# Filling five layer norms of a two-block transformer with quarters of a projection or value product

## What is computed

```python
for i in range(DEPTH):                       # first block
    m = mla_mixer(x, ...) if i % 2 == 0 else gla_mixer(x, ...)
    x = layer_norm(DN_ALPHA * x + m, ln1_g[i], ln1_b[i])
    x = layer_norm(DN_ALPHA * x + conv_ffn(x, ...), ln2_g[i], ln2_b[i])
    gate = jax.nn.sigmoid(x @ ple_w_gate[i] + ple_b_gate[i])
    x = x + gate * (p[i] @ ple_w_proj[i])    # the projection: needs p alone
...
for l in range(DEPTH):                       # second block
    h = layer_norm_2(DEEPNORM_ALPHA * h + 0.5 * swiglu(h, ...), ...)
    mix = short_conv(h, ...) if l < N_A else forgetting_attention(h, w_q, w_o, k, v, c)
    h = layer_norm_2(DEEPNORM_ALPHA * h + mix, ...)
    h = layer_norm_2(DEEPNORM_ALPHA * h + 0.5 * swiglu(h, ...), ...)
    if l == N_A - 1:
        k, v, c = shared_kv(h, kv_w, f_bias) # used by the attention of layer 1
```

## Time and profile before

| | us |
|---|---|
| median of 3 runs | 1794.31 (1794.29 to 1795.25) |
| the profiled execution, its own time | 1793.77 |
| its span, first to last instruction | 1791.9 |
| mean granted clock of TensorE, share of full | 0.999 |

### The profile page before, as it was taken

The page is one execution under the profiler, slowest core; times in us unless marked ns, Lnnn a source line. Parts: engine busy times, 40 slices in busy tenths (PEclk is TensorE's granted clock), DMA queues, the critical chain, the costliest instruction groups (busy, mean ns, idle before and its releaser), DMA issues.

```text
span 1791.9 us, 32993 instructions
## 1 busy us (share of the span) xinstructions
PE 1770.7 (99%) x14168; PEld 1735.1 (97%) x14168; DVE 1134.4 (63%) x1835; ACT 969.8 (54%) x1531; POOL 117.9 (7%) x124
## 2 busy tenths in 40 slices
PE   8999999999999999999999999999999999999998
PEld 8999999997899999999999999999999999899998
DVE  6776888565479885755546665554655556765554
ACT  5665766466367664744435454443554444764443
POOL 1001000110020001100011020001100002020002
PEclk9999999999999999999999999999999999999999
DMA  6424455544345555455444445555444554245552
GB/s 213 144 95 153 170 182 185 187 166 158 125 142 193 186 186 186 155 185 176 177 176 153 173 143 182 176 176 177 153 170 165 188 184 158 95 162 182 186 188 95
DMA packets 85056, 297.74 MB, mean 166 GB/s; under 512 B 10512, under 2 KB 13456, under 8 KB 84912
## 3 DMA queue, kind: packets, MB, share of 16 engines
q1 hardware_dynamic: 84176, 294.85, 47.2%
q10 hardware_dynamic: 736, 0.80, 0.1%
HBM read 294.57 MB, written 1.05 MB: 165 GB/s over the span
## 4 chain that ended last, share of the span: by engine, by line
PE 92%; DVE 3%; ACT 2%; DMA 1%; issue 1%; SPq 0%; POOL 0%; ACTq 0%; DVEq 0%; POOLq 0%
PE ps L1433 27%; PE ps L1431 27%; PE ps L1432 27%; PE ps L1462 2%; PE ps L1467 2%; PE ps L1463 2%; PE ps L1484 1%; DVE w_lo L888 1%; PE ps L1442 1%; DMA par<-params 1%; PE ps L1699 1%; PE ps L1701 1%; ACT x L462 1%; ACT w_hi L424 0%; PE ps L1898 0%
## 5 line engine op out<-in xcount | busy, mean ns | idle before, releaser
L888 DVE TENSOR_TENSOR w_lo<-raw,w_hi 128x1024 fp32r<-128x1024 f32 x557 | 689.6, 1246 | 348.7 <-ACT w_hi L424 226.6
L424 ACT ACTIVATE w_hi<-raw 128x1024 fp32r<-128x1024 f32 x557 | 580.6, 1051 | 178.1 <-DMA raw<-stream 155.5
L1431 PE MATMUL ps<-a_hi,w_hi 128*128 128x256 f32 (+1 forms) x2088 | 595.5, 285 | 5.7 <-DVE w_lo L888 5.5
L1433 PE MATMUL ps<-a_hi,w_lo 128*128 128x256 f32 (+1 forms) x2088 | 592.9, 284 | 0.0
L1432 PE MATMUL ps<-a_lo,w_hi 128*128 128x256 f32 (+1 forms) x2088 | 592.4, 284 | 0.0
L1431 PEld LDWEIGHTS ps<-a_hi,w_hi 128*128 128x128 f32 x2088 | 394.9, 189 | 7.9 <-DVE w_lo L888 7.1
L1433 PEld LDWEIGHTS ps<-a_hi,w_lo 128*128 128x128 f32 x2088 | 395.3, 189 | 0.0
L1432 PEld LDWEIGHTS ps<-a_lo,w_hi 128*128 128x128 f32 x2088 | 393.3, 188 | 0.5
L1431 PE MATMUL ps<-h_hi,w_hi 128*128 128x256 f32 (+1 forms) x1336 | 379.4, 284 | 0.3 <-DVE w_lo L888 0.3
L1433 PE MATMUL ps<-h_hi,w_lo 128*128 128x256 f32 (+1 forms) x1336 | 378.0, 283 | 0.0
L1432 PE MATMUL ps<-h_lo,w_hi 128*128 128x256 f32 (+1 forms) x1336 | 377.4, 282 | 0.0
(11 more groups left out here) (266 smaller groups left out, 1855.8 us busy)
## 6 DMA issues: line engine op xcount, KB each, us to landing
raw<-stream SPq DMA_DIRECT2D x557, 512.0 KB, 3.3
x<-xT SPq DMA_DIRECT2D x2, 512.0 KB, 5.0
out<-x SPq DMA_DIRECT2D x8, 128.0 KB, 1.7
work<-pT ACTq DMA_DIRECT2D x2, 256.0 KB, 2.6
par<-params SPq DMA_DIRECT2D x1, 283.5 KB, 11.2
tmp<-causal ACTq DMA_DIRECT2D x1, 208.0 KB, 2.4
con<-consts SPq DMA_DIRECT2D x1, 194.5 KB, 9.5
tmp<-pos SPq DMA_DIRECT2D x1, 128.0 KB, 9.5
```

The lines of the kernel that those rows point to most:

```text
L424: nc.scalar.activation(w_hi[:, u % SLOTS, :], raw[:, u % SLOTS, :], ACT.Copy).then_inc(w_hi_ready, 1)
L888: nc.vector.tensor_tensor(w_lo[:, u % SLOTS, :], raw[:, u % SLOTS, :], w_hi[:, u % SLOTS, :].bitcast(F32), ALU.subtract).then_inc(w_lo_rea ...
L1431: nc.tensor.matmul(dst, wh, xh, start=first, stop=False, skip_group_check=True)
L1433: return nc.tensor.matmul(dst, wl, xh, start=False, stop=last, skip_group_check=True)
```

## The change

Five norms (mla, ffn0, gla, ffn1, ffn4) get one unit each in four quarters of six matmuls. The units `proj0` and `proj1` are parted: unit a goes from the end of the network into the norm mla or gla, unit b stays in ffn0 or ffn1. The eighth unit of `kv_v` goes into the norm ffn4 (`kv_w`); its values are turned and copied in the attention. In these norms keep_busy is gone, the order of the sums is another ("sums first"), and DVE takes the reciprocal ahead of the first subtraction (`covered`). p is loaded and split ahead of `mla_ob` and `gla_o`; the splits of the weights move one unit ahead there. POOL adds seven tiles in gla. Network 4 closes with two units like 0 and 1, and in all three the last residual stands ahead of the last `lo_next`.

```diff
-           ("kv_k", 8), ("kv_v", 8), ("kv_f", 1),
-           ("up4", 44), ("down4", 22), ("att_q", 8), ("att_o", 8), ("up5", 44), ("down5", 22)]
+           ("kv_k", 8), ("kv_v", 7), ("kv_f", 1),
+           ("up4", 44), ("down4", 22), ("kv_w", 1), ("att_q", 8), ("att_o", 8), ("up5", 44), ("down5", 22)]
...
+COVERED_FFNS = (0, 1, 4)
...
-        pooled_of = {name: 6 if name in ("gla", "att") else 7 for name in LN}
+        pooled_of = {name: 6 if name == "att" else 7 for name in LN}
...
@@ ACT, layer_norm @@
+                    if k == LN["ffn4"] and n in (0, 2, 4):
+                        act.wait_ge(late_read, n // 2 + 1)
...
@@ ACT, order of the stages @@
+            load_p(0)
             warm(ACT.Sqrt)
-            plain("mla_ob", LN["mla"], TOK)
+            plain("mla_ob", LN["mla"], TOK, 0)
             layer_norm(LN["mla"], TOK)
-
-            load_p(0)
+            projected(0, 0)
             ffn(0)
-            projected(0, 0)
-            layer_norm(LN["ffn0"], TOK, BASE["proj0"] + 1)
+            layer_norm(LN["ffn0"], TOK)
             projected(0, 1)
...
             layer_norm(LN["ffn4"], TOK)
+            nc.scalar.activation(vT[:, 1, :], ps[:, 4, 0:T], ACT.Copy).then_inc(vT_copied, 1)
             warm(ACT.Exp)
...
@@ DVE, layer_norm @@
-                dve.wait_ge(mean_spread, k + 1)
-                lessened = [less_mean(0)]
+                lessened = []
+                if not covered:
+                    dve.wait_ge(mean_spread, k + 1)
+                    lessened.append(less_mean(0))
                 dve.wait_ge(std_ready, k + 1)
                 nc.vector.reciprocal(spread, spread).then_inc(rstd_ready, 1)
-                lessened += [less_mean(1), less_mean(2)]
+                dve.wait_ge(mean_spread, k + 1)
+                for n in range(len(lessened), 2 if covered else 3):
+                    lessened.append(less_mean(n))
...
                 scaled(1)
+                if covered:
+                    lessened.append(less_mean(2))
...
@@ DVE, end of a network @@
-                    lo_next(last + 1)
...
                 evict(1, 3)
+                if f in COVERED_FFNS:
+                    lo_next(last + 1)
...
@@ DVE, plain; alike on ACT @@
+            def plain(phase, k, cw, embedded=None):
                 for i in range(3):
                     lo_next(BASE[phase] + i)
+                if embedded is not None:
+                    split_p(embedded)
                 for i in range(KD):
                     u = BASE[phase] + i
                     dve.wait_ge(unit_done, u + 1)
                     residual(k, i, u % BANKS, cw)
-                    if i >= 3:
+                    if 3 <= i < (8 if embedded is None else 6):
                         lo_next(u)
+                    if embedded is not None and i >= 5:
+                        lo_next(u + 1)
...
@@ TensorE, the covered norms @@
+            def stats_over(k, part, late_pool):
+                if late_pool:
+                    part(0)
+                    sums(k, TOK, 7, "mean last pooled")
+                else:
+                    sums(k, TOK, 7, "pooled mean last")
+                    part(0)
+                if late_pool:
+                    part(1)
+                spread(k, TOK, 7, row_mean, mean_ready, mean_spread)
+                part(2 if late_pool else 1)
+                spread(k, TOK, 6, row_var, rstd_ready, rstd_spread)
+                if not late_pool:
+                    part(2)
+                part(3)
...
-            stats(LN["mla"], TOK, 7)
+            stats_over(LN["mla"], projection(0, 0), False)
             ffn(0, a_hi, a_lo, "ln0")
-            project(0, 0, (0, 1, 2, 3))
-            sums(LN["ffn0"], TOK, 7)
-            project(0, 1, (0, 1))
-            spread(LN["ffn0"], TOK, 7, row_mean, mean_ready, mean_spread)
-            spread(LN["ffn0"], TOK, 6, row_var, rstd_ready, rstd_spread)
-            project(0, 1, (2, 3))
+            stats_over(LN["ffn0"], projection(0, 1), True)
```

More of the change, by code:

```diff
@@ L88 @@
 CONV_FFNS = (0, 1)
+COVERED_FFNS = (0, 1, 4)
+PROJ = {(l, i): BASE[f"proj{l}{'ab'[i]}"] for l in range(2) for i in range(2)}
 ATT_Q_BANK = (0, 1, 2, 0, 1, 0, 1, 0)
@@ L793, in _ @@
                 hi_next(u)
-            for n in range(8):
+            for n in range(7):
                 u = BASE["kv_v"] + n
@@ L1473, in stream_product, with sums @@
                 each_unit(phase, whole(cw, src_hi, src_lo), dict(PHASES)[phase] - n_units, n_units)
-            def sums(k, cw, pooled):
+            def sums(k, cw, pooled, order="mean pooled last"):
                 blocks = token_blocks(cw)
@@ L1489, in pooled_squares @@
                     pe.wait_ge(sums_ready, 2 * k + 2)
-                    column(1, acc2, sum_place(cw)[0] != 6)
+                    return column(1, acc2, sum_place(cw)[0] != 6, order == "mean last pooled")
                 pe.wait_ge(sums_ready, 2 * k + 1)
                 column(0, acc1, True)
+                if order == "pooled mean last":
+                    pooled_squares()
                 for n in range(pooled, KD):
@@ L1520, in stats, with projection, part, late_values @@
                 keep_busy(6)
+            def stats_over(k, part, late_pool):
[13 more added lines that the diff above has]
+                part(3)
+            def projection(l, i):
+                def part(q):
+                    u = PROJ[l, i]
+                    pe.wait_ge(w_lo_ready, u + 1)
+                    pe.wait_ge(p_split, 2 * (l + 1))
+                    dst = ps[:, 4 + q // 2, (q % 2) * SEQ:(q % 2 + 1) * SEQ]
+                    for k in range(2):
+                        ins = three(dst, *tile(u, 2 * q + k), b_hi[:, k, TOK], b_lo[:, k, TOK], k == 0, k == 1)
+                    if q == 3:
+                        ins.then_inc(unit_done, 1)
+                return part
+            def late_values(q):
+                u = BASE["kv_w"]
+                pe.wait_ge(w_lo_ready, u + 1)
+                for k in (2 * q, 2 * q + 1):
+                    ins = three(ps[:, 4, 0:T], *tile(u, k), a_hi[:, k, 0:T], a_lo[:, k, 0:T], k == 0, k == KD - 1)
+                ins.then_inc(unit_done if q == 3 else late_read, 1)
             def spread_c(t):
@@ L1575, in ffn @@
                     ins.then_inc(unit_done, 1)
-                    closing = (1, 2 if f in CONV_FFNS else 3)[half]
+                    closing = (1, 2 if f in COVERED_FFNS else 3)[half]
                     each_unit(f"down{f}", down, 10 - closing, 11 * half + 1)
```

128 lines of the change are left out of this document (62 added, 66 removed).

## The result

| | before | after |
|---|---|---|
| median of 11 runs each, us | 1795.19 | 1801.11 |
| ratio | | 1.0032, 95% interval 1.0023 to 1.0041 |
| profiled execution, its time and span, us | 1793.77, 1791.9 | 1800.92, 1798.7 |

The forecast was 1796.9, the range ended at 1799.5. By the medians the change costs 5.9 us, not 2.6. Of the miss of 4.2 us, 0.9 is only that the kernel before measures 1795.19 over more runs instead of 1794.31.

The account below looks back on a forecast made before the run. It took TensorE, busy 99% of the span, as the bound, with POOL, DVE and ACT late around the norms. Terms summed to +2.6 on 1793.77, so 1796.4; with 0.54 for the median, 1796.9 us, range 1788.5 to 1799.5.

Parts of the forecast that it names:

- F to O: Each filled norm, from the first matmul behind the sums to the first of the next opening: 3.47 us, TensorE-bound.
- kv_v, mla and ffn4: Three terms: kv_v one unit and turn shorter, -3.35 us; last useful matmul to opening, mla +0.3, ffn4 +1.6.
- rival 1: Norm gla: TensorE's 3.7 us pause cuts the clock to half, +1.5 us, 1798.4 in all; chance 0.27.
- the walk: Norm gla: turns of DVE and POOL followed step by step, opening at 536.9 instead of 533.18, +3.7 us.
- ffn1: Norm ffn1: POOL free at y[6], moved split after it, opening at 727.7 instead of 729.63, -1.9 us.
- up0, up1, openings: ACT's copies start networks 0 and 1 each 1.0 us later, +2.0; third subtraction in the norms' openings, +0.4.
- The gates: gate1 and what follows: 0 us; gate0 with the gla mixer: only +0.35.
- p's subtractions: Before norm gla: two subtractions push the first residual from 515.30 to about 516.0, 0.35 us of gla's loss.
- The attention: Three transposes come back and TensorE waits for ACT's copy of vT: 0.3 + 0.4 = +0.7 us.
- rival 4: Whole kernel: Rival 2 together with ACT's copies being hidden, 1786.8 us; chance 0.08.
- Rival 2: Filled norms: POOL keeps up, last useful matmul to opening 5.4 or 6.2 us, 1788.8 in all; chance 0.16.
- the rule of the prediction: DVE and POOL alternate: addition 0.73 us alone, 1.60 with a split; a split meeting an addition ends 1.08 behind it.

Follow-up runs that it names:

- h4_late7: Changed kernel with gla's quarters and sums in the order of ffn1 (a quarter ahead, acc2 last), POOL's seven tiles kept: 1.0024 of the kernel before.
- g1_same: Changed kernel profiled once more with nothing edited: 1803.0 us, one run.
- e1_busy: Changed kernel with keep_busy in TensorE's waits for POOL, 15 matmuls in gla, 9 each in ffn0 and ffn1: 1.0024 of the kernel before.
- e2_gla6: Changed kernel with gla done in ffn1's order (a quarter ahead of the sums, acc2 last) and six POOL tiles instead of seven: 0.9998 of the kernel before.
- e3_copies: Changed kernel with ACT's copies of unit a moved behind the 17th unit of up0 and up1: 1.0016 of the kernel before.
- g3_comb: Changed kernel with the edits of e2_gla6 and e3_copies, and the copies of unit b moved behind the third gate unit: 0.9984 of the kernel before.
- h2_bgate: Kernel before with one edit, the copies of unit b moved behind the third gate unit: 0.9988 of the kernel before.
- h3_sixffn: Changed kernel with six POOL tiles instead of seven in ffn0, ffn1 and ffn4 alone: 1.0016 of the kernel before.
- g4_six: Changed kernel with six POOL tiles instead of seven in gla, order of sums and quarters kept: 1.0019 of the kernel before.
- g2_lolast: Changed kernel with both last splits of networks 0, 1 and 4 put behind the last residual: 1.0012 of the kernel before.

## Why the prediction was wrong

- **Sign and structure** were right: slower, with gla as the largest loss, five norms filled at 0.3 each, the saved unit of kv_v given back. F to O was put at 3.47 and measured 3.36 in mla, 3.34 in ffn1 and h4_late7. kv_v, mla and ffn4 came within 0.15, ffn4 by luck: with late loads it took 8.26 instead of 6.86 (g1_same).
- **The clock in gla** was rival 1 and was held the less likely. I took the one case of the earlier trace rows (a pause of 3.06, then 0.50) as thin evidence. The bracket in gla is 3.27, and in all five profiles with it the clock was cut. At full clock and in the same order gla took 8.95 (e1_busy), so POOL was even 0.3 us less late than the 9.2 of the walk, and the clock cost 1.3, near rival 1's 1.5. The step that failed is the weighing: the pause was predicted at 3.7 us by my own sum, above the only pause known to cut.
- **The clock in ffn0** was not thought of. The prediction itself says that TensorE stands still from 375.4 to 377.4 there; it read the earlier trace rows as a threshold near 3 us. It cost 1.55 in this execution (9.64 against 8.09), in one of the five with such a pause.
- **ffn1** was the mis-sized term: -1.9 predicted, -0.71 measured. The walk took POOL as free at y[6] and the moved split as coming after. That is the early state of the loads (6.8, so -2.0, measured in e2_gla6, e3_copies and g3_comb). The loads were late in this execution and the split came first. The step that failed is to read the turns of DVE and POOL from one execution as if the time of a load's landing were fixed. The earlier trace rows already came from the late state and the earlier trace rows from the early one; I did not ask why. With 6.8 in both norms, as in e2_gla6, the profiled execution would have been some 4 us shorter, an estimate from these rows, and inside the range: on which side of its end the number fell hung on a state that the prediction did not know of.
- **up0, up1, openings**: the mechanism was right (the wait of 0.92 on `w_lo`, gone in e3_copies) and the price too. The openings of mla, gla and ffn4 took 0.25 more each, 0.75 where I had 0.4.
- **The gates** were put at nothing. In gate0 matmuls start 0.45 and 0.62 apart at two places before and 1.06 apart at one place after, and with the longer opening each gate takes 0.3 more. g3_comb showed the pauses to be ACT's copies of unit b, which stood in the kernel before too. The other 0.2 of gate0 and the gla mixer is the fifth unit of `gla_o`, which starts 0.55 later against the opening than before, where I had charged 0.35 to p's subtractions.
- **The attention** cost 1.05 instead of 0.7: transposes 0.36, ACT's copy of vT 0.35, and 0.3 in the opening, which I had left among the unplaced.
- **A slip**: by its own terms (-5.6 and -2.4) rival 4 is 1786.4, not 1786.8. Nothing hangs on it.

Rival 2, that POOL keeps up, came near in the ffn norms in some executions (6.8 from E to O, where it had 6.2), and in gla in no run with seven tiles.

## What to carry to other kernels

Filling a wait with real work is worth little where another engine sets the end of that wait: first ask which engine delivers last, and give it less to do (POOL's six tiles instead of seven in three filled norms took the kernel from 0.9984 to 0.9965, with intervals that just overlap; filled with seven it could not be told from h2_bgate, which is not filled any further than before). Where dummy work is removed, the longest pause that is left is to be compared with every pause in the trace after which the clock fell, and one such case is enough to weigh it heavily. It doesn't settle the matter: the same pause had either outcome here. And where three engines take turns behind a load, read the same norm in several executions, or several norms of one kind in one execution, before the turns are taken as fixed.

## What the runs showed of the hardware

- **Loads have two states.** In the networks the 512 KB loads land 3.0 to 3.5 or 4.1 to 4.5 us after issue, with few between, and many in a row are alike (medians of 30 us stretches, 3.3 or 4.3). The state can change inside a network, both ways: in network 1 of h3_sixffn the medians from 550 us on are 4.3, 4.2, 3.3, 3.3, 3.2 and 4.2. The same kernel has both from execution to execution. No wait of TensorE in the filled norms is ended by a load; only the order of DVE and POOL shifts. What starts the late state is open.
- **The clock.** In the norms, the bracket of 3.27 to 3.29 in gla was followed by the half clock in five profiles of five (four kernels). Pauses of 1.9 to 2.6 by the bracket were followed by 0.50 once (ffn0 after) and not in eleven other cases, h4_late7's 2.59 among them. Two waits of 0.84 and 0.95 with one sum between them were followed by it too (g4_six), and in the gla mixer of h3_sixffn it came after waits of 0.51 and 0.56. The row behind the second wait, and the window of the half clock:

```profile
413.65 0.50 PE L1452 MATMUL ps<-w_hi,b_hi 128*128 128x512 f32 x1 [0.56 <-ACT tmp L697]
414.09:417.50 3.41, 3.41 (x10) 2.62 (x9) 3.24 (x4) 3.40 (x4) 0.00 (x0) 0.50 0.48 153
```

The other way round, the pause of the earlier trace rows, 3.06 us before, is 3.04 in after, and there the clock stayed whole behind it (row and window):

```profile
29.09 0.39 PE L1452 MATMUL ps<-a_hi,w_hi 128*128 128x256 f32 x1 [3.04 <-DVE w_lo L896]
29.10:32.50 3.40, 3.40 (x29) 3.40 (x30) 3.23 (x9) 3.39 (x8) 1.45 (x1) 1.00 0.00 0
```

Eleven profiles have this pause (3.04 to 3.09), and in two of them, after and e3_copies, the clock is 1.00 behind it. So the length of one pause doesn't decide alone. The half clock had begun when TensorE resumed in gla, and came 1.1 us behind the first sum in ffn0. From the end of the pause in gla it lasted 2.9 to 3.4 us in four profiles and 5.6 in g2_lolast. The Trainium skill (TensorE: Matmul & The Clock Gate, "The HAM clock gate") has the clock at two levels, the low one after idle time, and the point at which it rises varying from run to run. The traces agree on the levels (0.50 and 1.00 alone) and on the varying rise; why it fell after waits as short as those of g4_six and h3_sixffn no run here shows.
- **Turns of DVE and POOL** followed the rule of the prediction in the norms ffn0 of after, g1_same and e2_gla6: an addition free of splits took 0.73, one that met a split ended 0.6 behind it (1.59 in after, up to 1.8 where both were issued together), and a split that met an addition ended 1.1 behind that (1.71 in e2_gla6).
